# One core, two transformer blocks: an expert's scatter one chunk later, and the router's places counted ahead of its weights

## The reference

```python
def moe_ffn(h, router_w, w1, w3, w2):
    logits = (h @ router_w).astype(jnp.float32)
    top_vals, top_idx = lax.top_k(logits, TOP_K)
    top_w = jax.nn.softmax(top_vals, axis=-1)
    gate = jnp.sum(jax.nn.one_hot(top_idx, N_EXPERTS) * top_w[..., None], axis=-2)
    out = jnp.zeros_like(h)
    for e in range(N_EXPERTS):
        out = out + gate[..., e:e + 1] * swiglu(h, w1[e], w3[e], w2[e])
    return out
...
mod = c_act @ ada_w[l] + ada_b[l]      # second block: a row of 6 x 1024 for each layer
```

## Time and profile before

| | |
|---|---|
| median of 3 runs (lowest, highest) | 2449.72 us (2448.32, 2453.65) |
| the profiled execution, time | 2448.74 us |
| its span | 2446.9 us |
| PE busy | 2150.1 us, 88% |
| VectorE (DVE) busy | 1561.0 us, 64% |
| ScalarE (ACT) busy | 1196.8 us, 49% |
| mean granted TensorE clock | 0.933 |
| first to last matmul of the experts | 976.3 to 1780.6 us |

### The profile page before, as it was taken

The page is one execution under the profiler, slowest core; times in us unless marked ns, Lnnn a source line. Parts: engine busy times, 40 slices in busy tenths (PEclk is TensorE's granted clock), DMA queues, the critical chain, the costliest instruction groups (busy, mean ns, idle before and its releaser), DMA issues.

```text
span 2446.9 us, 25557 instructions
## 1 busy us (share of the span) xinstructions
PE 2150.1 (88%) x10570; PEld 1760.5 (72%) x10570; DVE 1561.0 (64%) x1586; ACT 1196.8 (49%) x1251; POOL 60.4 (2%) x87
## 2 busy tenths in 40 slices
PE   6888678998899775999999999999967699787997
PEld 5777456886788553878787787877756488576886
DVE  4565555554666643889888888888854455555443
ACT  5443224443644212777676676766723344333442
POOL 0000000000000000000000000000000100101000
PEclk9899889998999886999999999999988899898999
DMA  8355457556444336999999999999951665523551
GB/s 263 104 207 206 154 207 240 180 191 201 130 134 169 102 121 215 313 344 361 331 355 336 346 339 331 366 341 338 369 198 67 226 215 189 190 86 104 189 189 52
DMA packets 369318, 550.48 MB, mean 225 GB/s; under 512 B 21030, under 2 KB 295078, under 8 KB 362150
## 3 DMA queue, kind: packets, MB, share of 16 engines
q1 hardware_dynamic: 365168, 534.82, 64.9%
q10 hardware_dynamic: 4028, 13.95, 1.5%
HBM read 547.58 MB, written 1.15 MB: 224 GB/s over the span
## 4 chain that ended last, share of the span: by engine, by line
PE 80%; DVE 9%; ACT 5%; DMA 3%; issue 1%; POOL 1%; ACTq 0%; SPq 0%; DVEq 0%; POOLq 0%
PE bank L410 76%; DVE wlo L905 3%; PE bank L436 2%; ACT whi L899 2%; DMA raw<-in_moe_w 1%; POOL small L1938 1%; PE bank L485 1%; DVE scoresB L1426 1%; ACT xn L964 1%; DVE arena L1359 0%; DVE xn L1417 0%; DMA raw<-in_ada_w 0%; DMA xn<-in_lmask 0%; DVE outputs_lo L1731 0%; POOL small L1936 0%
## 5 line engine op out<-in xcount | busy, mean ns | idle before, releaser
L905 DVE TENSOR_TENSOR wlo<-raw,whi 128x2048 fp32r<-128x2048 f32 (+1 forms) x461 | 1052.3, 2287 | 442.9 <-ACT whi L899 442.3
L899 ACT ACTIVATE whi<-raw 128x2048 fp32r<-128x2048 f32 (+1 forms) x461 | 878.4, 1908 | 420.6 <-PE bank L410 359.5
L410 PE MATMUL bank<-whi,hThi 128*128 128x512 f32 (+2 forms) x1104 | 440.5, 399 | 29.0 <-DVE wlo L905 21.6
L410 PE MATMUL bank<-wlo,hThi 128*128 128x512 f32 (+2 forms) x1104 | 432.2, 391 | 0.0
L410 PE MATMUL bank<-whi,hTlo 128*128 128x512 f32 (+2 forms) x1104 | 431.3, 391 | 0.0
L410 PE MATMUL bank<-whi,slots_hi 128*128 128x512 f32 x704 | 283.4, 403 | 1.9 <-DVE slots_lo L1714 1.9
L410 PE MATMUL bank<-whi,slots_lo 128*128 128x512 f32 x704 | 278.4, 395 | 0.0
L410 PE MATMUL bank<-wlo,slots_hi 128*128 128x512 f32 x704 | 278.3, 395 | 0.0
L410 PEld LDWEIGHTS bank<-whi,hThi 128*128 128x128 f32 x1104 | 214.9, 195 | 76.1 <-DVE wlo L905 24.4
L410 PEld LDWEIGHTS bank<-whi,hTlo 128*128 128x128 f32 x1104 | 213.8, 194 | 43.5
L410 PEld LDWEIGHTS bank<-wlo,hThi 128*128 128x128 f32 x1104 | 214.4, 194 | 41.5 <-issue 0.8
(11 more groups left out here) (289 smaller groups left out, 2346.7 us busy)
## 6 DMA issues: line engine op xcount, KB each, us to landing
raw<-in_moe_w SPq DMA_DIRECT2D x352, 512.0 KB, 5.9
raw<-in_moe_w SPq DMA_DIRECT2D x88, 1024.0 KB, 7.6
raw<-in_w_in SPq DMA_DIRECT2D x72, 1024.0 KB, 5.3
raw<-in_ada_w SPq DMA_DIRECT2D x48, 1024.0 KB, 6.2
raw<-in_ffn_w SPq DMA_DIRECT2D x44, 512.0 KB, 5.0
raw<-in_w_gate SPq DMA_DIRECT2D x44, 512.0 KB, 4.0
raw<-in_w_up SPq DMA_DIRECT2D x44, 512.0 KB, 5.0
raw<-in_w_down SPq DMA_DIRECT2D x22, 1024.0 KB, 4.9
```

Source lines behind the costliest of these rows:

```text
L410: m = mm(dst, l_, r_, start=start and i == 0, stop=stop and i == len(pairs) - 1)
L899: s.then_inc(s.unit.activation(split_slot(whi, p)[:, 0:n], slot_of_ring(raw, p, NRAW)[:, 0:n], ACT.Copy), ("hi", p), sem="weights_hi")
L905: e.then_inc(e.unit.tensor_tensor(split_slot(wlo, p)[:, 0:n], slot_of_ring(raw, p, NRAW)[:, 0:n], split_slot(whi, p)[:, 0:n].bitcast(F32), ...
```

## The change

Three things. In the list of steps between chunks, an empty step goes ahead of the two scatters of each expert. In the router, VectorE makes `taken8` from the indices at once and the gates in a function of its own (`gates`), which runs behind `pick`; ScalarE's Exp goes ahead of its modulation row; TensorE runs four modulation pieces ahead of the places and four behind them. And `mod_row_spare` moves to memory that `put` shares, so that the wait for `row_out` goes from `pick` (VectorE) to `put` (ScalarE).

```diff
+        first8 = tiny(NT * NE)
...
-        mod_row_spare = sb(way, "modulation_row_spare", 4 * BANK)[0:1, :]
+        mod_row_spare = sb(way, "modulation_row_spare", NT * NE * P + 4 * BANK)[0:1, NT * NE * P:]
...
-                queue += [("scatter", e, t) for t in range(NT)]
+                queue += [None] + [("scatter", e, t) for t in range(NT)]
...
-        behind_chunks = queue
+        behind_chunks = [z for z in queue if z is not None]
...
-                modulation(("late", l))
+                modulation(("late", l), slice(0, 4))
                 tri = const("tri")
                 bank = t.take("places")
                 t.wait_ge("chosen")
...
+                modulation(("late", l), slice(4, 8))
                 t.wait_ge("slots_known")
...
-                        s.wait_ge(("full", ("put", pair)))
+                        s.wait_ge(("full", ("put", pair)), ("row_out", 1, 1))
...
-                    modulation(("late", l))
                     s.wait_ge("weights_low")
                     s.then_inc(act(w12.rearrange("p (t n) -> p t n", t=NT)[:, :, 1], w12.rearrange("p (t n) -> p t n", t=NT)[:, :, 0], ACT.Exp),
                                "weights_exp")
+                    modulation(("late", l))
                     s.wait_ge("slots_known", "x_split")
...
+                v.own()
+                v.then_inc(vcopy(idf, idx[:, :]))
                 v.then_inc(tensor(w3_[:, :, 0], top3[:, :, 1], top3[:, :, 0], ALU.subtract), "weights_low")
                 v.own()
-                v.then_inc(vcopy(idf, idx[:, :]))
-                v.wait_ge("weights_exp")
...
                 for tt in range(NT):
-                    v.then_inc(scalar(taken8[:, e8(tt)], const("iota8"), idf[:, tt * NE:tt * NE + 1], None, ALU.is_equal))
+                    v.then_inc(scalar(first8[:, e8(tt)], const("iota8"), idf[:, tt * NE:tt * NE + 1], None, ALU.is_equal))
                     v.then_inc(scalar(lg[:, e8(tt)], const("iota8"), idf[:, tt * NE + 1:tt * NE + 2], None, ALU.is_equal))
                 v.own()
+                v.then_inc(tensor(taken8, first8, lg, ALU.add), "chosen")
                 v.wait_ge(("full", "places"))
...
+            def gates():
+                v.wait_ge("weights_exp")
+                v.then_inc(scalar(w3_[:, :, 2], w3_[:, :, 1], 1.0, None, ALU.add))
+                v.then_inc(v.unit.reciprocal(w3_[:, :, 3], w3_[:, :, 2]))
+                v.then_inc(tensor(w3_[:, :, 4], w3_[:, :, 3], w3_[:, :, 1], ALU.mult))
+                for tt in range(NT):
+                    v.then_inc(scalar(gate8[:, e8(tt)], first8[:, e8(tt)], w3_[:, tt, 3:4], None, ALU.mult))
+                for tt in range(NT):
+                    v.then_inc(stt(gate8[:, e8(tt)], lg[:, e8(tt)], w3_[:, tt, 4:5], gate8[:, e8(tt)], ALU.mult, ALU.add))
...
             def sparse_experts(l):
-                v.wait_ge(("row_out", 1, 1))
...
+                gates()
...
             def dense_experts(l):
+                gates()
```

More of the change, by code:

```diff
@@ L473, in two_features, with modulation @@
                 t.then_inc(m, ("full", name), read)
-            def modulation(place):
-                for l, c, k in mod_chunks.get(place, []):
+            def modulation(place, part=slice(None)):
+                for l, c, k in mod_chunks.get(place, [])[part]:
                     modulation_piece(l, c, k)
@@ L1671, in experts_router @@
                 w3_, top3 = (z.rearrange("p (t n) -> p t n", t=NT) for z in (w12, top))
+                v.own()
+                v.then_inc(vcopy(idf, idx[:, :]))
                 v.then_inc(tensor(w3_[:, :, 0], top3[:, :, 1], top3[:, :, 0], ALU.subtract), "weights_low")
                 v.own()
-                v.then_inc(vcopy(idf, idx[:, :]))
+                for tt in range(NT):
+                    v.then_inc(scalar(first8[:, e8(tt)], const("iota8"), idf[:, tt * NE:tt * NE + 1], None, ALU.is_equal))
+                    v.then_inc(scalar(lg[:, e8(tt)], const("iota8"), idf[:, tt * NE + 1:tt * NE + 2], None, ALU.is_equal))
+                v.own()
+                v.then_inc(tensor(taken8, first8, lg, ALU.add), "chosen")
+                v.wait_ge(("full", "places"))
+                places = v.bank("places")
+                v.then_inc(reduce(most[0:1, :], places[0:1, 2 * NE:3 * NE], AXX, ALU.max))
+                v.then_inc(tensor(slot_of, taken8, places[:, 0:NT * NE], ALU.mult), ("free", "places"))
+                v.own()
+                v.then_inc(vcopy(flag[0:1, :], most[0:1, :]), "slots_known")
+                v.own()
+            def gates():
+                w3_, e8 = w12.rearrange("p (t n) -> p t n", t=NT), lambda tt: slice(tt * NE, (tt + 1) * NE)
                 v.wait_ge("weights_exp")
@@ L1689, in experts_router @@
                     v.then_inc(stt(gate8[:, e8(tt)], lg[:, e8(tt)], w3_[:, tt, 4:5], gate8[:, e8(tt)], ALU.mult, ALU.add))
[L1690 to L1693, removed]
-                v.then_inc(tensor(slot_of, taken8, places[:, 0:NT * NE], ALU.mult), ("free", "places"))
-                v.own()
-                v.then_inc(vcopy(flag[0:1, :], most[0:1, :]), "slots_known")
                 v.own()
             def sparse_experts(l):
-                v.wait_ge(("row_out", 1, 1))
                 for tt in range(NT):
```

## The result

The changed kernel takes 2414.17 us in the median of 4 runs (2412.06 to 2417.55), the kernel before 2450.41 in the same job: a ratio of 0.985, with a 95% interval of 0.9836 to 0.9864, or 36 us less. In a second job it was 2413.52 against 2452.64, 0.9841 (0.9826 to 0.9856), 39 us less. The forecast was 2410, in a range of 2403 to 2426.

The account below looks back on a forecast made before the run. The prediction took PE to bound the expert stretch, with DMA close behind. From 2448.74 us it took 8.1 (router), 20.2 (pauses) and 12.7 (clock), added 0.5 (VectorE), 1.0 (DMA) and 1.0 (median): 2410 us, range 2403 to 2426.

Parts of the forecast that it names:

- Router, 8.1 us: Router of layer 1: first expert matmul at 968.2 in place of 976.30, a gain of 8.1 us.
- the lower bound of 0: Router: no gain if taking the branch costs ScalarE the 9.5 us it idles ahead of `slots_hi`.
- its 1.16: Router: 1.16 us between the end of PE's places and the first `pick`, kept in the forecast.
- Pauses, 20.2 us: Seven expert boundaries: PE's waits for an expert's outputs go, 22.0 - 1.8 = 20.2 us.
- clock, 12.7 us: Seven scatter chunks directly behind the waits: 76.4 us falls to 7 x 9.10, 12.7 us less, going with the pause.
- VectorE at the boundary, 0.5 us: Expert boundaries: VectorE's split ends about when PE wants it; 0.07 us lost each, 0.5 in all, bounds 0 and 5.
- DMA, 1.0 us: Expert stretch: loads just keep up; 1.0 us lost for one disturbance, bounds 0 and 15.
- The rival of a lower ceiling: Expert stretch: long-time DMA ceiling of say 355 GB/s, 7 or 8 us more, 2418; chance 0.04.
- the argument that the lead needs the pauses of the kernel before: Experts: DMA falls behind 0.16 us a chunk and the 4.7 us pause refills that; without it, it just holds.
- The clock through the load: Experts: the granted clock stays at 1.00 through them.
- The rival of the other side: Experts: unbroken PE work brings half clock mid-load, 8.4 us more a chunk, 2460 from six chunks; chance 0.03.
- The sum: Whole kernel: 2448.74 - 8.1 - 20.2 - 12.7 + 0.5 + 1.0 = 2409.2, with 1.0 for the median 2410 us.

Follow-up runs that it names:

- Eight pieces ahead: The changed kernel with all eight modulation pieces ahead of the places, as before the change: 2417.50 us, 0.9858 of the kernel before.
- the scatter alone: The kernel before with only the scatter one chunk later, without the router's changes: 2423.94 us, 0.9883 of the kernel before.
- The added matmuls: The kernel before with ten 128x512 matmuls added in each of the seven pauses ahead of the first scatter: 2441.23 us, 0.9959 of the kernel before.
- the scatter inside the chunk: The changed kernel with each expert's first scatter between the up and down matmuls of its chunk: 2412.93 us, 0.9845 of the kernel before.
- four buffers: Four raw buffers in place of five, in the changed kernel (2438.89 us) and in the kernel before (2482.00 us).
- the router alone: The changed kernel with the scatter put back where it was: 2444.90 us, 0.9966 of the kernel before.
- changed, again: The changed kernel, nothing altered, timed and profiled again in a second job: 2413.52 us, 0.9841 of the kernel before.

## Why the prediction was right

**Router, 8.1 us.** R shrank by 8.3 (8.4 in the second profile), by the chain that was written down: landing of the second expert piece, its split, the row copies, bank 7. The third gather began 2.7 us behind the second, forecast were 2.8. ScalarE stands 0.99 us between its row copies and the first `slots_hi` (the row at 965.18), in which it issues the store, loads the count and branches, so the lower bound of 0 didn't come in. VectorE takes more for the branch than the prediction read: 0.72 us lie between the cast of the count and `pick`, not under 0.2, but they were inside its 1.16. What the prediction didn't see is that the division of the modulation matters; it has no price for it. Eight pieces ahead gives back 3.1 us.

**Pauses, 20.2 us, and clock, 12.7 us.** The sum held: the scatter alone takes E down by 30.1. But not all of the 12.7 is the clock. The added matmuls bring back 11.0, and each of the seven chunks keeps 0.3 over 9.10 at the full clock, about 2 us in all. That part shows behind each of these stops, with the slow clock or without it: the matmuls of a stream that doesn't stop overlap their neighbours, and at a stop this overlap is lost. In the changed kernel the stream still stops at each boundary, if shortly, so the part comes back in the next term. With that term as measured the sum is exact: 20.2 + 12.7 - 2.8 = 30.1.

**VectorE at the boundary, 0.5 us.** This is the term that was mis-sized: 2.8 us. The place was right. VectorE, then TensorE's weight loads (PEld), then its matmuls in the changed kernel:

```profile
1277.14 1.28 DVE L1738 TENSOR_TENSOR outputs_lo<-bank,outputs_hi 128x512 fp32r<-128x512 f32 x2
1278.34 0.41 DVE L1651 TENSOR_TENSOR gatedTlo_moe_sparse<-bank,gatedThi_moe_sparse 128x256 fp32r<-128x256 f32 x1
1278.67 4.48 DVE L907 TENSOR_TENSOR wlo<-raw,whi 128x2048 fp32r<-128x2048 f32 x2
...
1280.47 0.19 PEld L411 LDWEIGHTS bank<-whi,slots_lo 128*128 128x128 f32 x1
1281.17 0.19 PEld L411 LDWEIGHTS bank<-whi,gatedThi_moe_sparse 128*128 128x128 f32 x1 [0.52 <-issue]
...
1280.46 0.39 PE L411 MATMUL bank<-wlo,slots_hi 128*128 128x512 f32 x1
1280.69 0.39 PE L411 MATMUL bank<-whi,slots_lo 128*128 128x512 f32 x1
1281.20 0.47 PE L411 MATMUL bank<-whi,gatedThi_moe_sparse 128*128 128x512 f32 x1
1281.51 0.39 PE L411 MATMUL bank<-wlo,gatedThi_moe_sparse 128*128 128x512 f32 x1
```

The first of the last two splits ends near 1280.95, PE's 24 matmuls at 1281.08. By the prediction's count, from end to end, VectorE is in time, and the idle time of PE is only 0.13 us. The matmuls show why it costs more. In the stream they start every 0.23 us and overlap, and the weight load of each starts when the matmul before it starts (1280.47 for the matmul of 1280.69). So PE wanted the piece at about 1280.69, 0.26 us before the split ended; the load of the down products' first matmul ran at 1281.17. From 1280.69 to the next matmul it is 0.51 us and from there to the one behind it 0.31, in place of 0.23 each; the ones behind that are at 0.23 again. That makes 0.36 us, and the boundary costs 0.39 to 0.45 us, 2.8 in all. With the scatter inside the chunk E falls by just that.

**DMA, 1.0 us.** It cost nothing in these profiles: ScalarE has no wait for `raw` in the list of its waits in the experts. The landing time grew as forecast, here the highest row of the first profile, issued at 1369.1 near the end of the fourth expert (in the second profile the longest is 9.5 us):

```profile
raw<-in_moe_w SPq DMA_DIRECT2D x1, 1024.0 KB, 9.2
```

The rival of a lower ceiling is out for this kernel: the mean over the whole stretch is 357 GB/s, above the 355 it took, and 366 to 367 GB/s were held over seven chunks in a row in both kernels. By the 358 of the Trainium skill (DMA: Bandwidth & Descriptors, "Where 436 GB/s comes from") they couldn't be. One core ran here; what a second core at work would change, no run shows. Also out is the argument that the lead needs the pauses of the kernel before: without them no load came late, and with four buffers, where the lead is really short, the kernel with the pauses loses no less.

**The clock through the load.** 1.00 on the mean over 774 us; the only time at half clock lies behind PE's wait of 2.09 us near the end, from 1738.45 on. The rival of the other side didn't come.

**The sum.** From the first modulation piece to the last outputs the prediction has 8.1 + 32.9 - 1.5 = 39.5 us; the two profiles give 8.3 + 30.1 = 38.4. Of the missing 1.1 the boundary is 2.3 too little, against DMA's 1.0 too much and 0.2 more in the router. That the two ends of E cancel in the clock (1.6 us each way) is luck, and so is the 0.2: R of the unchanged router varies by more. By the medians the change is worth 36 and 39 us. Between single executions it can look like less, by what happens outside the stretch: in the first profile the unchanged code ahead of the router took 4.65 us more than in the kernel before and that behind the experts 2.5 more, so the execution was only 31.2 us shorter; in the second it was 1.5 and 2.5, and 34.4 us. Of the 4 us by which the first median is above 2410, 0.7 is the kernel before, which had 2450.41 there and not 2449.72; the rest isn't explained beyond this spread and the 1.1 above.

## What to carry to other kernels

A pause of PE costs itself and what comes slower behind it, here 2.9 us and on the mean 1.8, of which 0.3 is the stop itself and the rest the slow clock; read the chunk behind a wait against the same chunk elsewhere, and price both. When a wait goes, write out what the next engine still has to do up to PE's next need: count that need from the next weight load, which here was due 0.39 us ahead of the end of the last matmul, and not from that end. A stop of 0.13 us in the profile cost 0.4. And in a kernel whose waits pull other work in front of them (here two splits by a number in a table), the place of a wait in the order of all pieces counts as much as its place in an engine's program.

## What the hardware showed besides

- The same code ahead of the router takes different times. In the twelve profiles with five raw buffers the router's first modulation piece starts at 935.0 to 935.5 (four), 936.6 to 936.9 (four) or 939.5 to 940.0 us (four); the busy times of VectorE and ScalarE ahead of it agree within about 1 us, and stretches of PE at half clock lie differently. They don't explain the groups by their amount: the time at half clock ahead of 930 us is longest, 160 us, in the earliest (before), 150 in the latest (changed kernel) and 143 in the middle one (changed, again). The cause stays open. Behind the experts it is 663.5 to 668.1 us from the last outputs_lo to the end of the span. So one span says little about 3 us. R and E, measured between two events, say more: R is 32.5 to 32.7 us in the four profiles with the changed router and nothing else in it, and E is 775.0 or 775.1 in four with the scatter one chunk later, in which the clock costs 1.6 us at one of the two ends. But E moves by up to 2.9 us with the clock at the ends, and R of the unchanged router was 40.3 to 41.6.
- How much clock a pause costs isn't fixed by its length: the seven pauses of 2.9 to 3.0 us cost 0.3 (no half clock behind it) to 3.1 us, one of 8.5 us cost 2.5, and the wait of 1.93 us ahead of the first expert matmul cost nothing in the changed kernel and 2.7 us with the router alone.
- DMA brought 366 to 367 GB/s over 59 us (seven plain chunks in a row), at a share of 1.07.
